# A weight ring of a two-layer trunk kernel: the buffers of the modulation sums become a seventh slot, and TensorE's overflow branch moves by one pair

## The reference

```
mod = silu(c) @ w_ada + b_ada                # six rows of 1024: sh1 sc1 gt1 sh2 sc2 gt2
u = x*(1+sc1) + sh1;  proj = u @ w_in        # mLSTM heads and a gated short convolution
x = LN(alpha*x + (1+gt1) * (mixed @ w_out))
u = x*(1+sc2) + sh2
route: top-1 of 4 groups, then top-2 of its 4 experts, weights comb
y = sum over 16 experts of comb_e * (silu(u @ w_gate_e) * (u @ w_up_e)) @ w_down_e
x = LN(alpha*x + (1+gt2) * y)
```

## Time and profile before

| | |
|---|---|
| median of 3 runs | 845.73 us (843.96 to 846.73) |
| the profiled execution | 848.54 us, of it span 846.7 us, mean granted TensorE clock 0.985 |
| TensorE (PE) busy | 799.8 us (94%), 3788 matmul records |
| VectorE (DVE) busy | 418.5 us (49%) |
| queue of SyncE's transfers | 291.60 MB, 88.9% of 16 DMA engines' span |
| HBM | 297.60 MB read, 353 GB/s over the span |

### The profile page before, as it was taken

How to read it: one execution, slowest core, us unless ns; L and a number is a source line. 1 busy time by engine, 2 the same in 40 slices (tenths; PEclk the granted TensorE clock), 3 DMA queues, 4 the chain that set the end, 5 groups by cost and what they waited for, 6 DMA issues and landing times.

```text
span 846.7 us, 9216 instructions
## 1 busy us (share of the span) xinstructions
PE 799.8 (94%) x3788; PEld 420.0 (50%) x3810; DVE 418.5 (49%) x869; ACT 101.3 (12%) x237; POOL 28.9 (3%) x72
## 2 busy tenths in 40 slices
PE   8999999999999999999879999989899999999974
PEld 3485687445344434443338658844534443444321
DVE  0189888974423332333064985676442333233315
ACT  2111100023011001100111100002201000100010
POOL 2000000700000000000000000000000000000000
PEclk9999999999999999999989999999999999999997
DMA  9998998995999999999998599376399999999991
GB/s 317 389 387 319 388 386 310 366 391 214 382 410 414 416 410 413 415 412 411 410 389 306 213 358 386 136 258 242 146 376 415 414 414 410 414 414 410 414 405 56
DMA packets 90653, 299.29 MB, mean 353 GB/s; under 512 B 4152, under 2 KB 4440, under 8 KB 82416
## 3 DMA queue, kind: packets, MB, share of 16 engines
q1 hardware_dynamic: 86960, 291.60, 88.9%
q0 software_dynamic: 2592, 7.04, 2.2%
q10 hardware_dynamic: 1056, 0.03, 0.1%
HBM read 297.60 MB, written 1.05 MB: 353 GB/s over the span
## 4 chain that ended last, share of the span: by engine, by line
PE 82%; DMA 9%; DVE 3%; issue 3%; ACT 1%; POOL 1%; SPq 0%; POOLq 0%; DVEq 0%; ACTq 0%
PE bank L629 21%; PE bank L585 16%; PE bank L653 11%; PE bank L616 7%; PE bank L602 7%; PE bank L810 7%; DMA ring<-in_w_up_dram 6%; PE bank L675 3%; DMA ring<-in_w_gate_dram 3%; PE bank L486 2%; PE bank L496 1%; PE bank L563 1%; PE bank L637 1%; PE bank L683 1%; ACT uT L905 1%
## 5 line engine op out<-in xcount | busy, mean ns | idle before, releaser
L585 PE MATMUL bank<-uT,ring 128*128 128x256 f32 x640 | 140.4, 380 | 0.0
L585 PEld LDWEIGHTS bank<-uT,ring 128*128 128x128 f32 x640 | 121.0, 190 | 19.6 <-issue 3.6
L629 PE MATMUL bank<-ring,uT 128*64 128x512 f32 x512 | 114.0, 595 | 9.1 <-DMA ring<-in_w_up_dram 5.8
L629 PE MATMUL bank<-ring,qT 128*64 128x512 f32 x512 | 113.3, 594 | 3.0 <-issue 2.8
L653 PE MATMUL bank<-ring,hb 128*64 128x512 f32 x512 | 113.4, 595 | 1.4 <-ACT hb L931 1.4
L1055 DVE SCALAR_TENSOR_TENSOR acc<-ring,cond,acc 128x512 f32<-128x512 f32 x112 | 84.2, 752 | 4.0
L629 PEld LDWEIGHTS bank<-ring,uT 128*64 128x64 f32 x512 | 35.9, 137 | 81.5 <-issue 67.0
L629 PEld LDWEIGHTS bank<-ring,qT 128*64 128x64 f32 x512 | 36.7, 137 | 71.4 <-issue 68.8
L653 PEld LDWEIGHTS bank<-ring,hb 128*64 128x64 f32 x512 | 35.3, 137 | 71.6 <-issue 69.3
L1228 DVE SCALAR_TENSOR_TENSOR kT<-bank,share,gate_row 128x512 f32<-128x512 f32 x32 | 24.0, 749 | 90.0 <-PE bank L653 90.0
L616 PEld LDWEIGHTS bank<-ccT,X 128*128 128x128 f32 x512 | 61.5, 197 | 13.2 <-issue 11.4
(11 more groups left out here) (250 smaller groups left out, 600.9 us busy)
## 6 DMA issues: line engine op xcount, KB each, us to landing
ring<-in_w_gate_dram SPq DMA_DIRECT2D x32, 2048.0 KB, 18.5
ring<-in_w_up_dram SPq DMA_DIRECT2D x32, 2048.0 KB, 17.8
ring<-in_w_down_dram SPq DMA_DIRECT2D x32, 2048.0 KB, 17.4
ring<-in_w_ada_dram SPq DMA_DIRECT2D x24, 2048.0 KB, 18.4
ring<-in_w_in_dram SPq DMA_DIRECT2D x14, 2048.0 KB, 17.8
ring<-in_w_out_dram SPq DMA_DIRECT2D x4, 2048.0 KB, 15.4
gate_row<-in_b_ada_dram POOLq DMA_DIRECT2D x4, 512.0 KB, 6.7
ln_g<-in_ln_g_dram POOLq DMA_DIRECT2D x4, 512.0 KB, 7.4
```

The lines of the kernel that those rows point to most:

```text
L585: last = pe.matmul(bank[4 + (b0 + q) % 4][:, 0:SEQ], w[:, kc, q * P:(q + 1) * P], uT[:, kc, :], start=(kc == 0), stop=(kc == KC - 1))
L629: last = pe.matmul(bank[bk][CAP * j:CAP * (j + 1), :], xg[b][:, 4 * h + k, CAP * j:CAP * (j + 1)], ring[s[h]][:, 4 * j + k, :], start=(h = ...
```

## The change

- `acc` and `part` are now views of one new buffer `bench` of the size of a ring slot, which is appended to `ring` as slot 6. SBUF use stays the same.
- Slots are no longer `n % RING`. A queue `held` gives each block the slot that was filled longest ago; block `MOE[l] + 6` of each layer, the first gate block of pair 1, gets the bench. It waits for `row_ext >= 4l + 4` alone. From there on, a block of the experts waits for the block seven before it. When the bench's turn comes with a block of `STREAM`, the bench drops out.
- `gate2` moves from `acc` to `zT`, a buffer of the convolution that is idle by then.
- The overflow loops use slots 0 to 5.
- In the first layer, TensorE loads the flag and branches ahead of pair 7. With overflow, it runs pair 7 and its two last combine halves and then the loop; without, it jumps over both, meets a second `If(more == 0)`, and runs pair 7 and the last combine halves there. In the second layer the branch stays where it was.

```diff
+    SLOT, BEFORE, USE = [], [], []
+    held = deque((s, None) for s in range(RING))
+    for n in range(MOE[-1] + 6 * PAIRS):
+        s, prev = (RING, None) if n - RING in MOE else held.popleft()
+        if s == RING and n in UNIT_AT:
+            s, prev = held.popleft()
+        held.append((s, n))
+        USE.append(SLOT.count(s))
+        SLOT.append(s)
+        BEFORE.append(prev)
...
+        bench = sb("bench", [P, KC, COLS])
+        ring.append(bench)
...
-        acc = sb("acc", [P, GATE2 - 4, COLS])
-        gate2 = acc[:, 0:2, :].rearrange("p a n -> p (a n)")
+        acc = bench[:, 0:GATE2 - 4, :]
-        part = sb("part", [P, 2, COLS])
+        part = bench[:, GATE2 - 4:KC, :]
+        gate2 = zT[:, :, 2:2 + SEQ]
...
-                        released(sp, n - RING)
-                        expert_dma(sp, l, p, j, n % RING, landed[n % RING])
+                        if BEFORE[n] is None:
+                            sp.wait_ge(row_ext, 4 * l + 4)
+                        else:
+                            released(sp, BEFORE[n])
+                        expert_dma(sp, l, p, j, SLOT[n], landed[SLOT[n]])
...
+            def last_pair(l):
+                pair(l, PAIRS - 1)
+                for half in range(2):
+                    combine(main, PAIRS * (l + 1) - 1, (PAIRS - 1) % 2, half, last_pair=True)
...
-                for p in range(PAIRS):
+                for p in range(PAIRS - 1):
                     pair(l, p)
-                for half in range(2):
-                    combine(main, PAIRS * (l + 1) - 1, (PAIRS - 1) % 2, half, last_pair=True)
+                if l + 1 == DEPTH:
+                    last_pair(l)
                 more = pe.value_load(flag[0:1, l:l + 1])
                 with pe.If(more != 0):
+                    if l + 1 < DEPTH:
+                        last_pair(l)
...
+                if l + 1 < DEPTH:
+                    with pe.If(more == 0):
+                        last_pair(l)
...
-                        dve.tensor_scalar(gate2[:, cols], bank[4 + half][:, :], 1.0, None, ALU.add).then_inc(gate_row_ready, 1)
+                        dve.tensor_scalar(gate2[:, 2 * half:2 * half + 2, :], bank[4 + half][:, :].rearrange("p (q s) -> p q s", q=2),
+                                          1.0, None, ALU.add).then_inc(gate_row_ready, 1)
```

More of the change, by code:

```diff
@@ L15 @@
+from collections import deque
 from contextlib import ExitStack
@@ L194, in trunk_kernel @@
         dn_parts = [expo[:, :, :].rearrange("p h s -> p (h s)")[:, i * COLS:(i + 1) * COLS].bitcast(BF16) for i in range(3)]
-        landed = [sem(f"landed{i}") for i in range(RING)]
+        landed = [sem(f"landed{i}") for i in range(RING + 1)]
         x_landed = sem("x_landed")
@@ L268, in slot, with expert_slots @@
         def slot(unit):
-            return PLACE[unit] % RING
+            return SLOT[PLACE[unit]]
         def arrived(eng, kind, l, i):
             n = PLACE[kind, l, i]
-            eng.wait_ge(landed[n % RING], 16 * (n // RING + 1))
-        def expert_slot(l, j):
-            return (MOE[l] + j) % RING
+            eng.wait_ge(landed[SLOT[n]], 16 * (USE[n] + 1))
+        def expert_slots(l, p):
+            return [SLOT[MOE[l] + 6 * p + j] for j in range(6)]
         def expert_arrived(eng, l, j, p):
             n = MOE[l] + 6 * p + j
-            eng.wait_ge(landed[n % RING], 16 * (n // RING + 1))
+            eng.wait_ge(landed[SLOT[n]], 16 * (USE[n] + 1))
         def weighed_sums(l, i):
@@ L368, in _ @@
                             sp.dma_start(X[:, t, :], x[0, t * P:(t + 1) * P, :]).then_inc(x_landed, 16)
-                    if n >= RING:
-                        released(sp, n - RING)
-                    sp.dma_start(ring[n % RING][:, :, :], unit_source(unit)).then_inc(landed[n % RING], 16)
+                    if BEFORE[n] is not None:
+                        released(sp, BEFORE[n])
+                    sp.dma_start(ring[SLOT[n]][:, :, :], unit_source(unit)).then_inc(landed[SLOT[n]], 16)
                 for p in range(PAIRS):
@@ L385, in _ @@
                                 sp.wait_ge(over[l].down, 3 * (r * PAIRS + p))
-                                expert_dma(sp, l, p, j, expert_slot(l, j), over_landed[l][j])
+                                expert_dma(sp, l, p, j, j, over_landed[l][j])
                     sp.wait_ge(over[l].down, 3 * (ROUNDS - 1) * PAIRS)
@@ L693, in pair @@
                 n, b = PAIRS * l + p, p % 2
-                s = [expert_slot(l, j) for j in range(6)]
+                s = expert_slots(l, p)
                 pe.wait_ge(main.xg_act, n + 1)
@@ L860, in _ @@
                 pe.transpose(bank[5][0:1, 0:P], pmax[:, :], ident[:, :]).then_inc(pmaxT_done, 1)
-                for p in range(PAIRS):
+                for p in range(PAIRS - 1):
                     pair(l, p)
-                for half in range(2):
-                    combine(main, PAIRS * (l + 1) - 1, (PAIRS - 1) % 2, half, last_pair=True)
+                if l + 1 == DEPTH:
+                    last_pair(l)
                 more = pe.value_load(flag[0:1, l:l + 1])
                 with pe.If(more != 0):
+                    if l + 1 < DEPTH:
+                        last_pair(l)
                     S = over[l]
-                    s = [expert_slot(l, j) for j in range(6)]
+                    s = range(RING)
                     with pe.Fori(0, ROUNDS - 1) as r:
@@ L1076, in gate_row_2 @@
                 dve.wait_ge(gate_row_ready, 4 * l + 4)
-                link(dve.tensor_tensor(gate_row[:, :], gate_row[:, :], gate2, ALU.add))
+                row = gate_row[:, :].rearrange("p (q s) -> p q s", q=CH)
+                link(dve.tensor_tensor(row, row, gate2, ALU.add))
             def last_norm(l):
```

## The result

The changed kernel took 836.92 us (median of 4 runs, 834.03 to 838.65) beside 846.23 us for the kernel before (843.96 to 848.4): a ratio of 0.9887, interval 0.9843 to 0.993. The forecast was 836.9 us, in a range of 832.0 to 842.5, with 87% for faster. The kernel before ran once more here (848.4 us), which moved its median from 845.73 to 846.23. The profiled execution has a span of 836.9 us, where it was 846.7.

A forecast was written before the change was run, and what follows sets the result against it. The end of the weight stream was taken to bound each expert stage, with a branch stall at the layer border. Terms of -5.1, -0.3 and -3.4 sum to -8.8 us, from 845.73 to 836.9 us, range 832.0 to 842.5.

The forecast's parts named there:

- The second layer, -5.1: Second layer's experts: seventh block fetched in the pause, stream ends one block earlier, TensorE's waits go; -5.1 us.
- a lead of six blocks: Expert stages: TensorE begins six blocks ahead and loses about 2.6 us of it in each pair until pair 7.
- Pair 7 of the first layer: First layer: waits of 5.0 us go, branch standstill adds 2.8 and a clock fall 1.9; -0.3 us.
- The fall of the clock: First layer's pair 7: half clock after the 2.8 us standstill; +1.9 us, bounds 0 and 2.8.
- The border, -3.4: Between the layers: branch gone, TensorE then waits only for VectorE's `last_norm`; -3.4 us.
- A fall in the new idle stretch: Border's new idle stretches: none counted; would give back up to 1.9 us and mark the prediction wrong.
- The rest: `gate2` in `zT`, the second compare and the second layer's first blocks: costs nothing.
- The sum: Whole kernel: -5.1 - 0.3 - 3.4 = -8.8 us, subtracted from the median 845.73, giving 836.9 us.
- The rivals: Beside the main case (68%): cheap branch 10%, seventh slot moves nothing 8%, one more fetch 8%, slower 6%.
- the cheap branch: First layer's moved branch costs nearly nothing, pair 7 gains its 5.0 us; -13.5 us, 832.2 us; 10%.
- more blocks in flight would slow each other: Weight stream: possible reason that the seventh slot moves nothing; only the border gains, -3.4, 842.3 us; 8%.

The follow-up runs named there:

- e1: Changed kernel with TensorE's program put back, so only the seventh slot; 833.68 us, 0.9865 of the kernel before.
- after: The changed kernel with both parts, as first measured and profiled against the kernel before; 836.92 us, ratio 0.9887.
- e0: The changed kernel itself, run again beside the kernel before; 838.05 us, ratio 0.9911.
- e5: Changed kernel with eleven matmuls on zeros between pair 6 and the first layer's flag load; 838.03 us, 0.9909 of the kernel before.
- f0: The changed kernel repeated on one chip with the two variants that beat it; 837.94 us, 0.9914 of the kernel before.
- e7: Changed kernel with the zeros at program start cut into smaller pieces, 100 instructions more; one execution, 836.29 us, no ratio.
- e2: Kernel before, six slots, with only the first layer's branch moved ahead of pair 7; 843.67 us, ratio 0.9977.
- e4: Kernel before, six slots, branch not moved, only the border's eleven matmuls on zeros put ahead of the flag load; 843.55 us, ratio 0.9971.
- e6: Seventh slot alone, with the zeros at program start cut into smaller pieces, 100 instructions more; 0.9866 of the kernel before.
- e8: Seventh slot alone, its first block held back until TensorE has used the first gate block; 840.38 us, 0.9947 of the kernel before.
- f1: The seventh slot alone, repeated on one chip with the changed kernel; 834.2 us, 0.9871 of the kernel before.
- e3: Seventh slot, branch behind pair 7 as before, border's zeros put ahead of the flag load; 833.46 us, 0.9852 of the kernel before.

## Why the prediction was right, step by step

*The second layer, -5.1.* Measured 236.17 - 230.76 = 5.4 us. The mechanism held: one wait of 0.24 us for a transfer is left, and none with the slot alone (e1). That a stream which starts a block earlier ends a block earlier is right, but it was not as full as the prediction read it: its first 28 us ran at 366 GB/s. This did not touch the number, since one block more makes 5.1 us either way. One figure ahead of the sum is wrong and was not used in it: TensorE does not begin with a lead of six blocks, which would be 31 us. A loss of 2.6 us in each pair uses up some 18 us by pair 7, and the seventh block, issued at 201.86 and there by about 209, was wanted by pair 1 near 225.

*Pair 7 of the first layer.* The waits of 5.0 us went. The flag load was put at 390.7 and came at 390.7; the branch was taken at 6.19 us and took 6.07; gate was put at 397.9 and began at 397.64, a standstill of 2.49 us instead of 2.8. The fall of the clock was chosen on thin ground. It came, and cost 15.52 - 14.1 = 1.4 us where 1.9 were set. In six profiled executions with the moved branch it came in three (after, e0, e5) and not in f0, e7 and e2, though their standstills were no shorter (2.56, 2.54 and 2.45 us against 2.49, 2.45 and 2.12). So the reason given for it, that 2.8 us is nearly twice 1.47, predicts nothing here; the term is 1.4 us or nothing, and that it came in this profile is luck. Sum: 414.24 - 413.16 = -1.1 us, with -0.3 predicted.

*The border, -3.4.* Measured 170.94 - 167.66 = 3.3 us, both with an early fall. VectorE is now the late one, as said. The size of this term hangs on the clock too: against the slot alone, whose gap of 4.5 us was followed by half clock for 3.4 us instead of 6.8, the border gains only 168.07 - 166.3 = 1.8 us. The ratios of e2 and e4, 1.9 and 2.5 us, are nearer to this than to 3.4: the profile of the kernel before had the longest of these falls, and the prediction was wrong to say that nothing in its sum depended on that execution being 2.8 us above the median. A fall in the new idle stretch, counted as none, came in seven of the ten executions without the gap, though not in the profile of the result, and cost about 0.2 us (167.90 in e0 against 167.66 in after, both with an early fall). The prediction had named such a fall as a sign that it is wrong; by e0 and f0, which are the same kernel, that sign came.

*The rest.* The second compare took 0.078 us. `gate2` in `zT` left no trace.

*The sum.* -8.8 us predicted; the span went from 846.7 to 836.9 us, -9.8, and the median by 9.3. The mechanisms of all three terms held, and each size was off by less than 1 us. That the median hit the forecast to 0.1 us is luck: the four executions took 834.0, 835.2, 838.65 and 838.65 us, none near 836.9, and the median of the kernel before was 0.5 us higher than the one the forecast started from.

*The rivals.* None came true, but the cheap branch is real: e6 has it, by position. The prediction weighed it by the length of the jump and the traffic. What decides for a jump of the old length is where it starts. That more blocks in flight would slow each other is refuted: e8 ran faster with one more.

*What the prediction's own terms said and it did not say.* Its terms price the slot at -5.0 in each layer, and the moved branch at +2.8 + 1.9 - 3.4 = +1.3 us. Read so, they say that the second half of the change does harm once the first is there. The runs agree in sign (e1 and f1 against e0 and f0), and put the branch's standstill where nobody waits in e3.

## What to carry to other kernels

When a ring's stream is slower than its reader, what counts is when the stream starts: look for a pause ahead of it and for a buffer that is free by then, and look at the rate of the first blocks as well as at the last waits. Two remedies that both feed on one wait do not add; the branch that was free inside a wait for weights costs its full standstill once the wait is gone. A branch that may stall belongs where its engine would wait anyway, with work already queued ahead of it.

## What the runs showed of the hardware

- A branch of TensorE over the same loop body cost 0.35 or 6.25 us, by whether 100 instructions more stood ahead of it in the program. Each long one had a fetch of 16 KB of instructions inside it, no short one had. With idle DMA queues the long ones took 3.5 and 3.7 us, with full ones 6.0 to 6.3.
- TensorE's sequencer was 4.4 to 5.1 us ahead of its matmuls, an estimate of 34 to 43 instructions. Behind `down` 22 instructions more delayed it by 2.1 us; at the border, where it waits for VectorE, by 0.1 us.
- Standstills of 2.1 to 2.6 us were followed by half clock in three of six executions, one of 4.4 us by 6.8 us of it and ones of 4.1 and 4.5 us by 3.4 us.
- With blocks of 2 MB issued one by one as others were used, the stream began at 366 to 368 GB/s (mean of 28 us); with two issued at once, at 391 GB/s.
